# Down projections: the second half of each raw weight load on ScalarE's queue

## What is computed

```python
# first block
x = x + (jax.nn.gelu(u_gate) * u_val) @ w_ffn_down[i]
# second block
x = x + swiglu(rmsnorm(x, norm_ffn_g[layer]), w_ffn_in[layer], w_ffn_down[layer])
```

## Time and profile before

| | us |
|---|---|
| median of 3 runs | 2578.48 (2578.45 to 2578.59) |
| the profiled execution | 2578.38 |
| its span in the trace | 2576.6 |

### The profile page before, as it was taken

One profiled execution on the slowest core, in us unless ns is written; L12 is line 12 of the kernel. 1 busy time (PEld: TensorE's weight loads), 2 busy tenths in 40 slices (PEclk: granted clock), 3 DMA queues, 4 the chain that ended last, 5 costly groups with the idle time before them and its releaser, 6 DMA issues.

```text
span 2576.6 us, 34569 instructions
## 1 busy us (share of the span) xinstructions
PE 2560.8 (99%) x12410; PEld 2130.3 (83%) x12410; DVE 1693.3 (66%) x2069; ACT 1346.8 (52%) x1729; POOL 99.7 (4%) x110
## 2 busy tenths in 40 slices
PE   9999999999999999999999999999999999999998
PEld 8887788888888878888887888888888888888886
DVE  6656556877777778875667565465556554547887
ACT  5455546666555554555645466434544444444554
POOL 2000000111111100000000000000000000000000
PEclk9999999999999999999999999999999999999999
DMA  7745555666666575655655555655566666666564
GB/s 241 221 147 156 170 187 173 209 212 206 188 188 188 171 257 196 230 192 187 186 172 156 164 154 157 196 189 186 176 207 200 217 195 187 189 187 236 204 221 168
DMA packets 281420, 493.83 MB, mean 192 GB/s; under 512 B 14578, under 2 KB 123236, under 8 KB 281056
## 3 DMA queue, kind: packets, MB, share of 16 engines
q1 hardware_dynamic: 277952, 478.73, 59.2%
q0 software_dynamic: 3184, 13.41, 1.6%
q10 hardware_dynamic: 176, 0.27, 0.0%
HBM read 483.17 MB, written 9.18 MB: 191 GB/s over the span
## 4 chain that ended last, share of the span: by engine, by line
PE 95%; DVE 2%; DMA 1%; ACT 1%; issue 0%; SPq 0%; DVEq 0%; ACTq 0%
PE acc L757 19%; PE acc L759 19%; PE acc L758 19%; PE acc L1057 12%; PE acc L1050 6%; PE acc L1101 2%; PE acc L1103 2%; PE acc L1102 2%; PE tp L1101 2%; PE tp L1103 2%; PE tp L1102 2%; DMA RAW<-in_w_ffn_down_dram 1%; DVE SPL L2239 1%; ACT SPL L1625 1%; PE tp L785 1%; PE tp L848 1%
## 5 line engine op out<-in xcount | busy, mean ns | idle before, releaser
L1929 DVE TENSOR_TENSOR WL<-WR,WH 128x1024 fp32r<-128x1024 f32 x712 | 883.0, 1241 | 704.4 <-ACT WH L1379 703.0
L1379 ACT ACTIVATE WH<-WR 128x1024 fp32r<-128x1024 f32 x712 | 754.0, 1059 | 877.4 <-PE acc L759 717.1
L757 PE MATMUL acc<-WH,A 128*128 128x512 f32 x1328 | 523.7, 394 | 0.1
L759 PE MATMUL acc<-WH,A 128*128 128x512 f32 x1328 | 517.5, 390 | 0.0
L758 PE MATMUL acc<-WL,A 128*128 128x512 f32 x1328 | 517.1, 389 | 0.0
L1057 PE MATMUL acc<-A,WH 128*128 128x512 f32 x1408 | 336.4, 391 | 0.0
L1057 PEld LDWEIGHTS acc<-A,WH 128*128 128x128 f32 x1408 | 258.6, 188 | 50.0
L757 PEld LDWEIGHTS acc<-WH,A 128*128 128x128 f32 x1328 | 249.4, 188 | 53.7 <-issue 3.7
L759 PEld LDWEIGHTS acc<-WH,A 128*128 128x128 f32 x1328 | 249.3, 188 | 52.9
L758 PEld LDWEIGHTS acc<-WL,A 128*128 128x128 f32 x1328 | 249.6, 188 | 49.8
L1625 ACT ACTIVATE SPL<-RAW 128x1536 fp32r<-128x1536 f32 (+1 forms) x88 | 153.4, 1743 | 176.0 <-DMA RAW<-in_w_ffn_down_dram 78.8
(11 more groups left out here) (380 smaller groups left out, 3060.7 us busy)
## 6 DMA issues: line engine op xcount, KB each, us to landing
WR<-in_w_in_dram SPq DMA_DIRECT2D x199, 512.0 KB, 3.8
WR<-in_w_ffn_up_dram SPq DMA_DIRECT2D x176, 512.0 KB, 3.7
RAW<-in_w_ffn_down_dram SPq DMA_DIRECT2D x88, 1024.0 KB, 4.9
WR<-in_w_ffn_in_dram SPq DMA_DIRECT2D x176, 512.0 KB, 3.7
WR<-in_w_out_dram SPq DMA_DIRECT2D x64, 512.0 KB, 3.6
WR<-in_w_in_dram SPq DMA_DIRECT2D x65, 256.0 KB, 3.1
WR<-in_w_ple_gate_dram SPq DMA_DIRECT2D x32, 512.0 KB, 4.4
WR<-in_w_branch_a_dram SPq DMA_DIRECT2D x16, 512.0 KB, 4.0
```

Of the source, the lines that this page charges most:

```text
L757: pe.matmul(o, H[:, kt + k, cols], WH[:, s, k], start=begin, stop=False)
L759: mm = pe.matmul(o, L[:, kt + k, cols], WH[:, s, k], start=False, stop=end)
L1379: act.activation(WH[:, n % RING], WR[:, n % RING], ACT.Copy).then_inc(hi_done, 1)
L1929: dve.tensor_tensor(WL[:, n % RING], WR[:, n % RING], WH[:, n % RING].bitcast(F32), ALU.subtract).then_inc(lo_done, 1)
```

## The change

From the fifth group of each projection on (`by_halves`: groups 4 to 43 of the 44, 40 in each projection and 80 in all) SyncE's DMA brings the first k-tile only, 512 KB. The second k-tile, 512 KB, is brought by a DMA in ScalarE's list, written directly after the first rounding of the group ahead (`load_half` behind L1625), with the same wait for the raw buffer that SyncE has. Both ScalarE and VectorE (where it reads the raw buffer before the rounding) wait for a second semaphore, `half_in`. Nothing else is moved.

```diff
@@ -455,6 +455,7 @@
         raw_in = [sem(f"raw_in{n}") for n in range(ENTRIES)]
+        half_in = [sem(f"half_in{n}") for n in range(ENTRIES)]
@@ -497,6 +498,13 @@
+        def by_halves(q):
+
+            return q.n % (2 * PER_HALF) >= 4
+
+        def half_landed(q):
+            return half_in[q.entry], 16 * len([m for m in QUADS[:q.n + 1] if m.entry == q.entry and by_halves(m)])
@@ -592,7 +600,11 @@
             def load_raw(w, q):
                 if q.reused:
                     sp.wait_ge(q_lo, q.reused)
-                sp.dma_start(raw_of(q)[:], rows(w, 2 * q.j, summed_columns(q.half, 0, 2))).then_inc(raw_in[q.entry], 16)
+                kt, cols = 2 * q.j, summed_columns(q.half, 0, 2)
+                if by_halves(q):
+                    sp.dma_start(raw_of(q)[:, 0], w[kt * P:(kt + 1) * P, cols]).then_inc(raw_in[q.entry], 16)
+                else:
+                    sp.dma_start(raw_of(q)[:], rows(w, kt, cols)).then_inc(raw_in[q.entry], 16)
@@ -1619,11 +1631,15 @@
             def roundings(q):
                 split = split_of(q)
                 act.wait_ge(*raw_landed(q))
+                if by_halves(q):
+                    act.wait_ge(*half_landed(q))
                 if q.emptied[0]:
                     act.wait_ge(q_used, q.emptied[0])
                 blocks = raw_blocks(q)[:, 1:4] if q.seven else raw_blocks(q)
                 act.activation(split[:, q.slots[0]:q.slots[0] + (3 if q.seven else 4), 0, :], blocks,
                                ACT.Copy).then_inc(q_hi, 1)
+                if q.n % (2 * PER_HALF) + 1 < 2 * PER_HALF and by_halves(QUADS[q.n + 1]):
+                    load_half(QUADS[q.n + 1])
                 if q.seven:
@@ -1631,6 +1647,12 @@
+            def load_half(q):
+                w, kt = w_down if q.half < 2 else w_down2, 2 * q.j + 1
+                act.wait_ge(q_lo, q.reused)
+                act.dma_start(raw_of(q)[:, 1], w[kt * P:(kt + 1) * P, summed_columns(q.half, 0, 2)]
+                              ).then_inc(half_in[q.entry], 16)
@@ -2240,6 +2262,8 @@
                 dve.wait_ge(*raw_landed(q))
+                if by_halves(q):
+                    dve.wait_ge(*half_landed(q))
```

## The result

The changed kernel takes 2588.31 us (median of 7 runs, 2585.51 to 2591.18) against 2578.59 (2578.45 to 2581.0) for the kernel before. The ratio is 1.0035 with a 95% interval of 1.0025 to 1.0045: slower by 9 to 10 us, which is more than the 0.2% that can be told from no change. The profiled execution took 2591.18, so its trace shows a run 2.9 above the median; its span of 2589.4 is 12.8 longer than that of before.

What follows compares the result with a forecast made beforehand. TensorE was taken to bound the kernel, leaving at most 1.96 us to gain. The profiled 2578.38 + 0 (queues) + 0 (steady groups) + 0.5 (where STA is loaded) gave 2578.9 us; range 2576.5 to 2590.

Steps and rivals of the forecast that it cites:

- rival 2: Beside STA, two requests for 1 MB make halves land later than their share: +7, 2585.5 us; chance 0.10.
- What bounds the kernel, and no gain from it: In both projections TensorE sets the pace; no gain can exceed its idle time of 1.96 us, 0.08%.
- SyncE, ScalarE's queue: SyncE's 80 issues with half the bytes gain nothing; ScalarE's 80 added waits and issues of 0.45 us cost nothing.
- What orders a DMA behind a rounding: In ScalarE's queue, the issue doesn't wait for the running rounding's end; GpSimd's row spoke for waiting, which would give 2601 us.
- rival 1: The second half's issue waits for the rounding's end: 0.64 a pair, 22.5 us in all, 2601 us; chance 0.20.
- Rival 3: ScalarE's queue goes past the rounding's waits, so the half is issued with SyncE's: no change, 2578.4 us; chance 0.17.
- When the second half lands: In steady groups a half lands in 3.7 us, a seven's 0.4 later than before of an allowed 2.25; cost nothing.
- the break-even: In a steady pair, two landings and two starts fill TensorE's 10.23 us when a half takes 5.0 to land.
- The eight's half: In steady groups it waits for the remainder, goes out with SyncE's half and lands at 1071.3, unchanged; cost nothing.
- Where STA is loaded: In groups 4 to 10 of each projection, without slack, some landings slip by tenths: +0.5 us, bounds -1.96 and +7.
- Rival 4: The stalls vanish, as two queues issue at once and STA no longer delays the raw load: at most -1.96, 2576.5 us; chance 0.03.

Runs made afterwards that it cites:

- second experiment: Against the changed kernel, ScalarE still issues the second half, but ahead of the rounding's waits instead of behind the rounding; 2579.43 us, ratio 1.0 to the kernel before.
- first experiment: Against the changed kernel, SyncE issues both halves one after the other once the raw buffer is free, ScalarE none; 2579.0 us, ratio 0.9998 to the kernel before.

## Why the prediction was right, and where it was not

The range of 2576.5 to 2590 held the time. The point, 2578.9, was 9.4 low, and the likeliest verdict, no difference, was the wrong one: at a ratio of 1.0035 the result is in the 0.22 that I gave to slower. By the prediction's own terms that chance should have been larger: 0.20 + 0.10 less half of the 0.10 is 0.25, before anything is added for the forecast's own error. That the range held is partly luck: its upper end was set for rival 2, whose cause is not what the runs show.

- *What bounds the kernel, and no gain from it.* Right.
- *SyncE, ScalarE's queue.* Right. The issue takes 0.33 for the 0.45 taken, and nothing queued behind it is late (second experiment).
- *What orders a DMA behind a rounding.* Right: 0.03 after the rounding's start. This decided between forecast and rival 1. GpSimd's row didn't carry over to ScalarE. Here the trace agrees with the section of Perfetto Trace Analysis in the Trainium skill that was weighed there.
- *Rival 1's price.* Its mechanism was built by itself: 2618.5, not 2601. Its 22.5 us were little over half of the 39 that were lost: 10.87 lies between the shortest pairs (10.4 to 10.6) and the average (11.40), and it had no term for what lengthens the others.
- *Rival 3.* Out: the issues come 0.03 behind the rounding, not with SyncE's.
- *When the second half lands.* **This step failed.** "A half by itself lands in 3.7" is the median of 176 loads of 512 KB in another stage, and it was used for a half that shares the DMA engines with another, issued at the median 0.9 ahead of it. It measured 4.8, and 5.05 and 5.12 in the steady groups shown. So the seven was rounded 5.15 after the eight and not 3.8, and "all stays hidden" held in steady groups only because it came out on the break-even. The right row had been at hand: the raw load of 1 MB at 4.9, since both halves are the same megabyte on the same DMA engines. The break-even of 5.0 was right to the tenth (a turn is the landing and 0.10), and it was named as what would make the number wrong. I had 4.8 as the upper end, from a row for another reason, and called it hidden with a margin of 0.2 to the break-even.
- *The eight's half.* "Goes out with SyncE's at the remainder" didn't hold. Once sevens round 5.15 behind the eight, the buffer is free first (1068.98) and the half waits for the rounding (1069.87), so both groups of the pair turn in the loop. Of the 80 halves, 7 go out together with SyncE's.
- *Where STA is loaded.* The term was +0.5 with a bound of +7. The idle time grew from 1.15 to 4.18, so by 3.0. The argument, "the same bytes end at the same time", took a later issue for free, where the earlier trace rows had shown that nothing was in hand.
- *Missing: the other neighbours.* `PWR` (2.13) and `fw` (3.17) cost nothing before, when by the prediction's sums an eight's load had 1.3 in hand and a seven's 2.25. I worked out what a steady group could bear and spent it; I didn't ask who else had been living on that slack. That is 5.3 of the 8.35 us of added idle time in this execution.
- *Rival 2* came nearest in time (2585.5), with the wrong cause. Two requests cost nothing (first experiment), and the stalls are not only between 925 and 960.
- *Rival 4.* With both issues at once 0.9 of the 1.96 went in the profiled execution, which the time can't tell from nothing (ratio 0.9998); with the change nothing of it went.

## What to carry to other kernels

Before a DMA is hung behind a computing instruction, write down the loop that this closes, landing to instruction to issue to landing, and price it with the landing of the *whole* set of bytes that are under way together, not with that of a request of its size alone. If the loop comes within some tenths of the engine that sets the pace, the steady state may cost nothing and the other loads in the stretch can still cost time, here between 1 and 22 matmuls for the same load: list those loads, as their delays were paid from the slack that is spent. A buffer's refill is best issued when the buffer is free, on whichever queue; if part of it has to wait, let it be a small last part.

## What was not expected of the hardware

- How long a 512 KB load takes depends on how far behind another it is issued, on ScalarE's and SyncE's queue alike. The two halves of each group, paired in the order of their issues, give for the late one, at the median:

  | issued behind SyncE's half by | changed kernel | late half on SyncE's queue |
  |---|---|---|
  | 0.2 to 0.6 | 4.6 (19 halves) | 4.5 (26) |
  | 0.6 to 1.0 | 5.1 (19) | 5.2 (24) |
  | 1.0 to 1.5 | 4.8 (25) | 4.6 (23) |

  Issued behind the end of the rounding, 2.2 or more after SyncE's, it lands in 3.7 (78 halves). In both kernels the whole megabyte takes 5.0 from the first issue in the first row, and 6.0 in the second. Why it takes 1.0 more when the second issue comes only some 0.4 later stays open: the queueing explains that the late half waits, not this.
- A stall can cost more than its idle time. The first matmul behind one is booked longer, here in the changed kernel behind a stall of 2.13:

```profile
1087.23 0.50 PE L1113 MATMUL tp<-SPL,BH 128*128 128x512 f32 x1 [2.13 <-DVE SPL L2274]
```

  Back-to-back ones show 0.39. With the issue behind the rounding's end, the same 12,410 matmuls were busy for 2578.7, 17.9 more than before, beside 22.4 more of idle time (2616.9 - 2578.7 less 15.8). What of it is such restarts and what is the clock isn't separated.
- One stall of 2.7 us was followed by 4 us at a granted clock of 0.57 to 0.58. In the kernel with the late half on SyncE's queue it was 0.86 and 0.50 in the two stretches of 2 us (1090 to 1094) around and behind the end of a stall of 1.9. A stall of 2.1 in the same place of the changed kernel left it at 1.00. So the length of one stall didn't decide here.
